# Layer 0's expert search: inside the keys' loop, or behind it for eight heads at once

## What is computed

```python
q = (xc @ wq).reshape(C, PEER_HEADS, 2, PEER_DKEY // 2)          # 8 heads, 2 halves of 128
s = jnp.einsum('chzd,zkd->chzk', q, subkeys)                      # 128 scores for each half
top_s, top_i = lax.top_k(s, PEER_TOPK)                            # the 16 best of each half
cand_s = (top_s[:, :, 0, :, None] + top_s[:, :, 1, None, :]).reshape(C, PEER_HEADS, -1)
best_s, best_j = lax.top_k(cand_s, PEER_TOPK)                     # the 16 best pairs: the "search"
idx = jnp.take_along_axis(cand_i, best_j, axis=-1)
g = jax.nn.softmax(best_s, axis=-1)
act = jax.nn.gelu(jnp.einsum('cd,chkd->chk', xc, jnp.take(u, idx, axis=0)))
return jnp.einsum('chk,chkd->cd', g * act, jnp.take(v, idx, axis=0))
```

## Time and profile before

| what | us |
|---|---|
| median of 3 runs | 5116.07 |
| lowest and highest | 5114.26, 5117.12 |
| the profiled execution's own time | 5112.4 |
| its span, from first to last instruction | 5110.6 |
| DVE in layer 0's keys' loop, first to last instruction | 1036.34 to 1223.56 |
| first copy of the lots (L2090) in layer 0's experts' stage | 1293.51 |

### The profile page before, as it was taken

One profiled execution on the slowest core, in us unless ns is written; L12 is line 12 of the kernel. 1 busy time (PEld: TensorE's weight loads), 2 busy tenths in 40 slices (PEclk: granted clock), 3 DMA queues, 4 the chain that ended last, 5 costly groups with the idle time before them and its releaser, 6 DMA issues. The chain is left out here.

```text
span 5110.6 us, 54755 instructions
## 1 busy us (share of the span) xinstructions
PE 4353.6 (85%) x18847; PEld 2969.2 (58%) x18847; DVE 3399.7 (67%) x7418; ACT 1214.6 (24%) x2191; POOL 1823.0 (36%) x1652
## 2 busy tenths in 40 slices
PE   7899986693888799999999977886747778999997
PEld 5577664382555566667666644552533435666765
DVE  2366665578878777776777745664687775666665
ACT  2222311110444311111111122331213332222221
POOL 0022111022766555554555500000237774344331
PEclk9899978797999999999999989997878989999998
DMA  6967775612999999999999927667338999999995
GB/s 231 312 184 218 206 212 160 211 45 80 367 376 364 356 372 352 360 360 342 369 354 361 358 92 226 173 187 222 119 102 330 351 341 351 356 356 359 357 357 192
DMA packets 514328, 1407.98 MB, mean 276 GB/s; under 512 B 45693, under 2 KB 128637, under 8 KB 509215
## 3 DMA queue, kind: packets, MB, share of 16 engines
q1 hardware_dynamic: 329758, 733.60, 44.1%
q0 software_dynamic: 184320, 671.17, 34.6%
HBM read 1226.33 MB, written 178.26 MB: 275 GB/s over the span
## 5 line engine op out<-in xcount | busy, mean ns | idle before, releaser
L1723 POOL DMA_INDIRECT expert_rows<-u_rows,peer_arena x640 | 885.1, 1383 | 1274.5 <-DVE expert_rows L2025 1035.9
L1768 PE MATMUL ps<-part_arena,peer_part_arena 128*128 128x384 f32 (+1 forms) x4096 | 1035.4, 335 | 29.8 <-DVE peer_part_arena L2068 27.9
L2025 DVE SCALAR_TENSOR_TENSOR expert_rows<-expert_rows,mixer_in 128x1024 f32<-128x1024 f32 x640 | 761.7, 1223 | 139.2 <-DMA expert_rows<-u_rows,peer_arena 127.2
L1730 POOL DMA_INDIRECT expert_rows<-in_peer_v,peer_arena x640 | 730.6, 1142 | 196.0 <-issue 182.8
L1740 PE MATMUL ps<-expert_rows,peer_arena 128*128 128x512 f32 x1024 | 530.4, 669 | 294.8 <-DVE peer_arena L2033 284.4
L1768 PEld LDWEIGHTS ps<-part_arena,peer_part_arena 128*128 128x128 f32 x4096 | 699.0, 190 | 92.7 <-issue 77.9
L1777 PE MATMUL ps<-best,peer_arena 128*128 128x512 f32 x1540 | 685.3, 592 | 0.0
L1768 PE MATMUL ps<-mixer_in_parts,peer_part_arena 128*128 128x384 f32 (+1 forms) x2048 | 633.2, 309 | 0.0
L1740 PEld LDWEIGHTS ps<-expert_rows,peer_arena 128*128 128x128 f32 x1024 | 209.1, 214 | 560.8 <-issue 307.8
L2052 DVE SCALAR_TENSOR_TENSOR peer_arena<-expert_rows,peer_arena 128x1024 f32<-128x1024 f32 x381 | 489.7, 1285 | 30.2 <-DVE peer_arena L2052 1.9
L1777 PEld LDWEIGHTS ps<-best,peer_arena 128*128 128x128 f32 x1540 | 285.0, 189 | 296.0 <-issue 296.0
(11 more groups left out here) (270 smaller groups left out, 6199.8 us busy)
## 6 DMA issues: line engine op xcount, KB each, us to landing
peer_arena<-in_peer_u SPq DMA_DIRECT2D x256, 512.0 KB
best<-in_peer_v SPq DMA_DIRECT2D x154, 512.0 KB
mixer_arena<-in_peer_u SPq DMA_DIRECT2D x272, 256.0 KB, 7.8
u_rows<-mixer_arena SPq DMA_DIRECT2D x136, 512.0 KB, 6.6
hidden<-in_peer_u SPq DMA_DIRECT2D x240, 256.0 KB, 6.3
u_rows<-hidden SPq DMA_DIRECT2D x120, 512.0 KB, 5.1
gates<-peer_arena SPq DMA_DIRECT2D x20, 2048.0 KB
peer_arena<-in_peer_v SPq DMA_DIRECT2D x52, 512.0 KB
```

What stands on the lines that cost most here:

```text
L1723: pool.indirect_dma_start(u_ring[:, k % U_SLOTS, :], None, u_table, bass.IndirectOffsetOnAxis(u_index[s][:, m:m + 1], 0)).then_inc(u_row_i ...
L1730: pool.indirect_dma_start(v_ring[:, k % V_SLOTS, :], None, v_table, bass.IndirectOffsetOnAxis(v_index[s][:, m:m + 1], 0)).then_inc(v_row_i ...
L1768: mm = pe.matmul(ps[:, 6, 0:dense_tok], left[j % len(left)][:, c, :], right[:, c, :], start=at == 0, stop=at == len(todo) - 1)
L2025: dve.scalar_tensor_tensor(out=rows, in0=rows, scalar=1.0, in1=B.x[:, :, rows_at + s * P:rows_at + s * P + P], op0=ALU.mult, op1=ALU.mult, ...
```

## The change

`SEARCHED` becomes `(0, 0)`: no tile is searched in layer 0's loop.

```diff
-SEARCHED = (2, 0)
+SEARCHED = (0, 0)
```

## The result

The changed kernel takes **5083.39 us** (median of 7 runs, 5070.47 to 5093.84), the kernel before beside it 5115.52 (7 runs, 5105.44 to 5129.27). The ratio is 0.9936, with a 95% interval of 0.9917 to 0.9954. The profiled execution of after took 5085.8 us.

The account below looks back on a forecast made before the run. DVE was taken to bound layer 0's keys' loop. Removing its search gains 34.6 us, less 9.7 and 3.3 for the two searches: 21.6 us less, 5116.07 to 5094.5 us, range 5088 to 5103.

Parts of the forecast that it names:

- The bound and the loop: Layer 0's keys' loop: DVE bounds it; without the search PE paces it at 9.68 us a projection, 34.6 us less.
- the 10 us of the old loop beyond its own sum: Layer 0's keys' loop took 187.2 us against 177.2 summed over heads; most of the rest put on L1548 meeting POOL's L1518.
- The passage and the two searches: Behind layer 0's loop: passage stays 3.03 us, first search in the open adds 9.67, second among the products adds 3.3.
- the gathers didn't pace the start: Rival in `choose(1)`: waits for gathered rows stay, second search costs 11.4 us, time 5102.6; chance 0.07.
- All later stages at their old length: From the first copy L2090 to the end, every stage keeps its length and starts 21.6 us earlier.
- Faster than 5088, by something that the rows don't show: Case for the whole kernel: time below 5088 us for a reason not in the profile rows; chance 0.05.
- the gather's shift: First gather behind layer 0's loop starts 24.9 us earlier; used for the lower end of the range.
- the test that I named: The forecast is wrong if the distance from L2090 to the end of the span isn't the old one.
- A loop with another pacemaker: Rival in layer 0's loop: something other than DVE holds its pace, searches add 13.0 us, time 5129.1; chance 0.04.
- an absorbed shift: Rival at the experts' stage: its end hangs on something that doesn't move, time within 10 us of before; chance 0.06.
- gathers that pace the lots: Rival in the experts' stage: lots follow the gather's start alone, 24.9 us earlier, time 5091.2; no chance of its own.
- The moved collision: Rival in layer 0's loop: L1548 meets L1518 in the last two projections, 4.3 us lost, time 5098.8; chance 0.10.

Follow-up runs that it names:

- the three sets: Three measurements of the changed kernel against the kernel before: ratios 0.9936, 0.9947 and 0.9950.
- the kernels with one tile: Changed kernel with SEARCHED (1, 0): one tile searched in layer 0's loop, the other behind `choose(0)`; 5106.98 us, 0.9979 against the kernel before.
- the split: Changed kernel with the first four heads' search put between two loops of four heads, the other four heads' search behind the loop; 5089.28 us, 0.9938 against before.

## Where the prediction was right, and which steps failed

**The bound and the loop: right.** DVE set the loop's end, and without the search PE does. PE's scores come every 9.68 us to the fifteenth, DVE waits about 1.26 us for PE at each projection up to that one, and the loop took 152.58 us for 152.6 predicted. That a good part of the 10 us of the old loop beyond its own sum was copies blocked by L1518 is shown by the kernel with both copies as reductions, which is 6.9 us shorter.

**The passage and the two searches: right.** 3.23, 9.68 and 47.13 us for 3.03, 9.67 and 47.11. The neighbours that carried these terms were layer 1's own rows of the same code. The kernel that does both searches twice shows their price without the loop's gain, 12.5 for 13.0. DVE no longer waits for gathered rows, and the gathers didn't pace the start: POOL's first one came at 1205.46, with no wait of DVE's behind it.

**All later stages at their old length: wrong.** The step of the mechanism that failed is "Nothing in it was waiting for something outside the stage, and so I carry the shift to the end at full size". A shift in time does carry to the end. But the sum has no term for what the edit changes in the pace of code behind it. It moved that code to another place in DVE's program, and a loop 2400 us later went from 106.65 to 102.00 us: its turn lost 0.13 us and its two long copies vanished. I had used that very loop's long copy as a rival, in the place where it would cost something, and didn't ask what it would take to go away where it already was: L1548 was late by 0.08 us. "Faster than 5088, by something that the rows don't show" had a chance of 0.05.

**The account.** 21.6 from the stretch, 4.65 from layer 1's loop, less 0.6 that its passage took more (6.12 for 5.50), make 25.6 us. Over the three sets the kernels differ by 27.4 ± 1.4, so 1.8 us are left, little more than the error. Layer 1's loop alone wouldn't have taken the time out of the range: 5116.07 - 25.6 = 5090.5. The first measurement's 32.1 us lie beyond that by the spread of the runs, as far as these runs can tell: its own standard error was 4.3.

**The range: wrong in its lower end.** I built it from the gather's shift and "the 3 us by which the runs of before differ". Three runs can't show the spread of 25 us. The stretch from L2090 to the first dense matmul differed by 12.5 us among profiles with the same work, so the distance from L2090 to the end of the span couldn't serve as the test that I named, either. It was 3817.1 us before and 3819.7 after: longer by 2.6 us, although layer 1's loop in it was shorter by 4.65. With a standard error of 4.3 us on the difference of seven runs and seven, several us either way were due for that alone.

**The other rivals: not borne out.** A loop with another pacemaker, an absorbed shift, gathers that pace the lots: the profiles of after have no sign of any: PE has no gaps in the loop, layer 0's stretch is at 235.5 us in three profiles, and DVE doesn't wait for gathered rows. The moved collision did appear, in the kernels with one tile (9.8 us) and with the split (3.7 us), where DVE is behind PE at least for a while.

**What stays open.** What ahead of a loop makes its turn 0.13 us longer; why layer 1's passage takes 6.1 us in all three profiles of after and 5.5 in both of before; and the gain of the kernel with one tile, 10.1 ± 2.5 where its profile accounts for 3.1.

## What to carry to other kernels

Work that is taken off the pacemaker of a loop gains only down to the pace of the next engine; price it from a stretch of the same trace in which that engine already leads, and price what is put back in the open from the rows of the nearest stage with the same code. Where two engines' times in a loop are within a per cent or two of each other (here 12.93 or 12.80 us against 12.70), a tenth of a us a turn can decide whether instructions collide, and an edit ahead of it can change that: look at such loops even if the edit is elsewhere, and try copies that don't collide. Don't take the spread of three runs (here 3 us) for the spread of a kernel (here 25 us).

## What was unexpected of the hardware

- A short stall of 0.12 to 0.13 us at the turn of a DVE loop, or at one projection within it, comes and goes with padding ahead of the loop. Layer 1's loop had none in after (102.00 us), one a head in before and in before with padding of 16, 32 or 64 (106.64), one and more meetings with POOL in after with 3 (109.81), and two in before with 61 (113.52). The stalls themselves are about 1 us each over the loop; the rest are copies that wait for POOL.
- A copy of 0.2 us that starts 0.08 us behind a POOL instruction of 2.40 us waits for the whole of it; one that ends 0.48 us ahead of it costs nothing. As a `tensor_reduce` it takes 0.25 us in layer 0, and none was long in any of the kernels that have it.
- When one of two such copies is changed to the form that doesn't wait, the wait moves to the other (median 0.93 us) and only 1.1 us of 6.9 are gained.
